# VectorE block transposes in place of TensorE transposes and ScalarE copies in the expert loop of a hybrid decoder step

## The reference, cut to what matters

```python
y = 0
for wg, wu, wd, ge in experts:              # 32 experts, D_MODEL 1024, EXPERT_FF 512
    h = silu(xt @ wg) * (xt @ wu)           # inner activations
    y = y + ge[:, None] * (h @ wd)          # ge: gate of each token for this expert, 0 for most
```

## Time and profile before

| what | value |
| --- | --- |
| time of three runs | 884.41, 885.39, 886.82 us, median 885.39 |
| span of the profiled execution, first to last instruction | 882.0 us |
| TensorE busy in it | 862.2 us (98%) |
| VectorE busy | 350.6 us (40%) |
| ScalarE busy | 180.2 us (20%) |
| expert loop | roughly 390 to 870 us of the span |

### The profile page before, as it was taken

How to read it: one execution, slowest core, us unless ns; L and a number is a source line. 1 busy time by engine, 2 the same in 40 slices (tenths; PEclk the granted TensorE clock), 3 DMA queues, 4 the chain that set the end, 5 groups by cost and what they waited for, 6 DMA issues and landing times.

```text
span 882.0 us, 13906 instructions
## 1 busy us (share of the span) xinstructions
PE 862.2 (98%) x5646; PEld 516.7 (59%) x5646; DVE 350.6 (40%) x816; ACT 180.2 (20%) x362; POOL 30.4 (3%) x89
## 2 busy tenths in 40 slices
PE   8999999999999999999999999999999999999996
PEld 6657777786677667674535553554455445535553
DVE  5476999755577663240102211220222022102214
ACT  3342002347312310131111111110111011101112
POOL 0001203300200000000000000000000000000000
PEclk9999999999999999999999999999999999999998
DMA  7333254114535138909999999999999999999951
GB/s 281 96 95 100 86 176 120 57 43 159 160 112 184 38 144 354 381 28 379 409 419 414 428 416 418 413 430 413 415 418 428 414 414 427 419 417 415 428 229 55
DMA packets 28822, 247.70 MB, mean 281 GB/s; under 512 B 3312, under 2 KB 5616, under 8 KB 16112
## 3 DMA queue, kind: packets, MB, share of 16 engines
q1 hardware_dynamic: 28784, 247.17, 70.6%
HBM read 242.23 MB, written 4.92 MB: 280 GB/s over the span
## 4 chain that ended last, share of the span: by engine, by line
PE 88%; DVE 7%; ACT 2%; DMA 1%; issue 1%; SPq 0%; DVEq 0%; ACTq 0%
PE psum L1121 38%; PE psum L561 13%; PE psum L1074 7%; PE psum L1156 7%; PE psum L572 5%; PE psum L1031 4%; PE psum L1002 1%; PE psum L1078 1%; DVE sb_arena L1692 1%; DVE sb_arena L1689 1%; PE psum L882 1%; PE psum L1139 1%; DMA sb_arena<-w_oab 1%; DMA sb_xT<-xT 1%; PE psum L717 1%
## 5 line engine op out<-in xcount | busy, mean ns | idle before, releaser
L1121 PE MATMUL psum<-sb_arena 128*64 128x512 f32 x1536 | 334.0, 593 | 1.5 <-ACT sb_arena L1462 1.0
L1121 PEld LDWEIGHTS psum<-sb_arena 128*64 128x64 f32 x1536 | 110.9, 136 | 212.6 <-issue 212.6
L2106 DVE TENSOR_TENSOR sb_arena<-sb_arena,psum 128x512 f32<-128x512 f32 x16 | 11.0, 688 | 304.5 <-PE psum L1121 304.5
L561 PE MATMUL psum<-sb_arena 128*128 128x313 f32 (+2 forms) x480 | 126.9, 423 | 0.0
L561 PEld LDWEIGHTS psum<-sb_arena 128*128 128x128 f32 x480 | 90.0, 190 | 34.5 <-issue 2.3
L2101 DVE TENSOR_TENSOR sb_arena<-sb_arena,psum 128x288 f32<-128x288 f32 x120 | 54.5, 454 | 74.8 <-PE psum L1156 71.0
L1074 PEld LDWEIGHTS psum<-sb_arena 128*128 128x128 f32 x544 | 62.0, 192 | 13.6 <-issue 13.0
L572 PE MATMUL psum<-sb_arena 128*128 128x288 f32 x256 | 66.5, 412 | 0.1
L1074 PE MATMUL psum<-sb_arena 128*128 128x128 f32 x544 | 65.2, 278 | 0.4 <-DVE sb_arena L2049 0.4
L1156 PE MATMUL psum<-sb_arena 128*128 128x288 f32 x240 | 61.3, 407 | 0.0
L1455 ACT ACTIVATE sb_arena<-psum 128x256 f32<-128x256 f32 x68 | 20.6, 389 | 179.0 <-PE psum L1078 179.0
(11 more groups left out here) (393 smaller groups left out, 736.4 us busy)
## 6 DMA issues: line engine op xcount, KB each, us to landing
sb_arena<-w_gu SPq DMA_DIRECT2D x64, 2048.0 KB, 15.2
sb_arena<-w_dn SPq DMA_DIRECT2D x32, 2048.0 KB, 11.1
sb_arena<-w_in SPq DMA_DIRECT2D x30, 512.0 KB, 3.6
sb_arena<-w_gab SPq DMA_DIRECT2D x16, 512.0 KB, 3.8
sb_arena<-w_oab SPq DMA_DIRECT2D x16, 256.0 KB, 3.1
sb_arena<-gdn_in SPq DMA_DIRECT2D x4, 512.0 KB, 5.2
sb_arena<-w_o SPq DMA_DIRECT2D x4, 512.0 KB, 6.2
sb_arena<-w_o SPq DMA_DIRECT2D x1, 2048.0 KB, 7.8
```

What stands on the lines that cost most here:

```text
L561: last = mm(bk(n % 2, N)[:, first_col(n):], w_ring[n % 2][:, k, :], (xw if n < 2 else xnT)[:, k, first_col(n):], start=(k == 0), stop=(k = ...
L1121: last = mm(bank[b][half, :], rows[:, k, half], weights(s, k), start=(at_ == 0), stop=(at_ == n_k - 1))
```

## The change

The seven transposes of a pair leave TensorE, and the two copies out of PSUM leave ScalarE. VectorE reads `hid_s` and `selG` in SBUF and writes `hidT` and `selT` in SBUF, in blocks of 32 by 32. One instruction takes 32 partitions and every block column of one kind: four blocks (128 elements per partition) for the activations, three or two blocks (96 or 64 elements) for the gates. Each of the two transposes takes 16 such instructions. `turn_hidden` stands ahead of the adds in VectorE's order, `turn_gates` behind them and ahead of `weigh`.

```diff
 # TensorE
-                    if not first:
-                        pe.wait_ge(S["selT"], i)
                     project(1, KD, xe, ...).then_inc(S["sp_up"], 1)
-                def turn_hidden(i):
-                    pe.wait_ge(S["sp_hid"], i + 1)
-                    for f in range(4):
-                        last = pe.transpose(bank[0][:, f * P:f * P + P], hid_s[:, f * P:f * P + P], K("ident"))
-                    last.then_inc(S["sp_ht"], 1)
-                def turn_gates(i):
-                    pe.wait_ge(S["sp_selg"], i + 1)
-                    for m in range(3):
-                        last = pe.transpose(bank[1][:, m * P:m * P + P], selG[:, m].rearrange("p s c -> p (s c)"), K("ident"))
-                    last.then_inc(S["sp_selT"], 1)
                     gather()
-                    turn_hidden(i)
                     if not first:
                         combine(i, i + 2)
-                    turn_gates(i)
                     down(i, first)
 # ScalarE
                     take(i + 1)
-                    act.wait_ge(S["sp_ht"], i + 1)
-                    A(hidT.rearrange("p k c -> p (k c)"), bank[0][:, :], ACT.Copy).then_inc(S["hidT"], 1)
-                    act.wait_ge(S["sp_selT"], i + 1)
-                    A(selT[:, :], bk(1, 3 * P), ACT.Copy).then_inc(S["selT"], 1)
 # VectorE
+                hid_b = hid_s.rearrange("p (f c) -> p f c", f=4)
+                def turn_hidden():
+                    for b in range(0, P, B32):
+                        for g in range(0, P, B32):
+                            ins = V.transpose(hidT[g:g + B32, :, b:b + B32], hid_b[b:b + B32, :, g:g + B32])
+                    ins.then_inc(S["hidT"], 1)
+                def turn_gates():
+                    to = selT.rearrange("p (m t) -> p m t", m=3)
+                    of = selG.rearrange("p m s c -> p m (s c)")
+                    for b in range(0, P, B32):
+                        n = 2 if b else 3
+                        for g in range(0, P, B32):
+                            ins = V.transpose(to[g:g + B32, 0:n, b:b + B32], of[b:b + B32, 0:n, g:g + B32])
+                    ins.then_inc(S["selT"], 1)
                 def pair(i, first):
                     ...
                     TT(hid_s, silu_s, bank[1][:, :], ALU.mult).then_inc(S["sp_hid"], 1)
+                    dve.wait_ge(S["sp_hid"], i + 1)
+                    turn_hidden()
                     if not first:
                         dve.wait_ge(S["sp_acc"], KD * (i - 1) + 2)
                         add(i)
-                    dve.wait_ge(S["sp_selT"], i + 1)
+                    dve.wait_ge(S["sp_selg"], i + 1)
+                    turn_gates()
+                    dve.wait_ge(S["selT"], i + 1)
                     weigh(i + 1)
```

## The result

The changed kernel takes 880.8 us (median), the one before 885.39: 0.9944 of it, 95% interval 0.993 to 0.9957, so 4 to 6 us faster. I had forecast 899.2 us, 1.6% slower, and 12% for faster. Of the five executions behind the 880.8, one lasted 4981.6 us, which nothing here explains; the other four took 879.31 to 881.83 us, and the ratio and its interval rest on them alone. The profiled execution has a span of 878.1 us, 3.9 less than before.

The account below looks back on a forecast made before the run. TensorE, busy 98%, was taken as the bound; 15 pairs x 0.82 us plus 1.5 for pair 0 gave +13.8 on the 882.0 span, 895.8, plus 3.4 to the median: 899.2 us, range 887 to 915.

Parts of the forecast that it names:

- What VectorE gets: Step pricing VectorE's 32 short block transposes per pair: 0.40 us per activation transpose, taken between 0.39 and 0.42.
- the prediction's own formula: Change per pair with a combine, 16p - 5.58 us: adds' slip less the gate saving; pair 0, 16p - 4.93.
- fixed part: Cost of each VectorE instruction whatever its length: 0.155 us, from elementwise rows, paid every time on part of the partitions.
- The path: Between gather and down projection: ScalarE's copies into `xe` hold combine 2; VectorE's transposes delay the adds that combine 4 needs.
- the activation part: Activation transposes leaving TensorE ahead of the combine: 0 gained in pairs 1 to 15, not 0.59 us.
- the gate part: Gate transposes leaving TensorE between combine and down projection: 0.33 us less per pair in 15 pairs, -4.9 us.
- the signs named for the profile after: Transposes every 0.40 us, ScalarE wait about 0.7, add wait near 1, period 30.9 us, `down` straight after combine, no weight waits.
- the begin of the slip: Combine 4 starts late, waiting for VectorE's first add, by 16p - 5.25 us per pair, positive from p = 0.328.
- cheap short transposes: Rival: p below 0.328 in VectorE's 4.73 us gap, combine 4 not late, 880.0 to 880.8 us; chance 0.10.
- nothing measurable: Rival: p between 0.34 and 0.36, adds' slip and gate saving cancel, 883 to 888 us; chance 0.05.
- Gate transposes on VectorE: After the adds, 16 short transposes taking 4.7 us per pair, covered by TensorE's projections, cost nothing.
- the case of the full 0.92 us: Rival: all TensorE transposes count, 14.7 us less, 870.7 us, but transfers hold it near 875; chance 0.02.

Follow-up runs that it names:

- the run with other shapes: The changed kernel plus block transposes of other shapes and strides into unused space at the end of VectorE's work for a pair: single time 884.28 us.
- the two runs with more transposes: The changed kernel plus two or six further 32x128 transposes per pair ahead of VectorE's sixteen: 887.27 us with two, 909.37 us with six.
- strided ones: The changed kernel with `hid_s` stored interleaved, so the sixteen activation transposes read neighbours four elements apart: 908.28 us, 1.0259 of the kernel before.
- The run with less to transfer: The kernel with six banks, loading only a quarter of the second expert's down weights in each pair after the first: 873.79 us, 0.9868 of the kernel before.
- four banks: The changed kernel with the combine writing banks (6, 7, 0, 1) in place of (6, 7, 2, 3): 879.06 us, 0.9931 of the kernel before.
- six banks: The changed kernel with the combine writing banks (6, 7, 0, 1, 2, 3, 6, 7): 874.44 us, 0.9875 of the kernel before.

## Why the prediction was wrong

**The step that failed is the size p of a short transpose** in "What VectorE gets": 0.40 us, when it is 0.316. In the prediction's own formula each hundredth of a microsecond above 0.328 counts 16 times in each of 15 pairs, and each one in pair 0 counts 16 times: 240 x (0.40 - 0.328) + 16 x 0.084 = 18.6 us, and the forecast of 899.2 lies 18.4 us above the measured 880.8. The size came from the earlier trace rows, whose instructions have the same operation, type and partitions. Their price per element, 1.73 ns, belongs to the stride in their access (`"p c h i -> p i (c h)"` in the code of lines 1701 and 1702), which the row doesn't print, and the new ones read and write runs of 32 adjacent elements. The code was there to be read, and the elementwise rows had the right price per element, 1.04 ns; with it and their fixed part the sum would have been 0.155 + 0.133 = 0.29 us, on the right side of 0.328. The prediction did weigh 1.04 ns per element, but took the 1.93 us of the long row for granted, so that all the rest had to be fixed part (0.87 us) and the case looked absurd. That the long row was dear for its access was not among the possibilities.

**The fixed part and the missing overlap were right.** The earlier trace rows gave 0.155 us and no overlap; measured are 0.17 and a gap of 0.013 us. The reason given, that instructions on a part of the partitions never overlap, is too wide: in the run with other shapes the two 32x512 on the same 32 partitions took 1.29 us together, less than 2 x 0.681. The sixteen of the change go to other partitions from each to the next.

**The path was right.** Combine 2 is held by ScalarE, the activation part gives nothing, the gate part 0.33 us per pair, and the adds are what would be late: all measured by parts. Of the signs named for the profile after, the longer wait for ScalarE came (0.62 us, forecast 0.7), `down` follows the last combine at once, and no load of the loop waits for weights; the wait for an add and the period of 30.9 us, which hung on p, did not come. The formula put the begin of the slip at p = 0.328; the two runs with more transposes put it at 0.316 + 0.30/16 = 0.335.

**The rival "cheap short transposes" came true**: 0.316 lies below its deciding point, 0.328. It had a median of 880.0 to 880.8 us; measured is 880.8. The two traces agree with its terms: the loop is 15 x 0.33 = 4.9 us shorter, pair 0 cost about 0.1 more (from the issue of the gate weights to that of the down weights 20.33 us in place of 20.24), and the loop began 0.8 us later in this execution, before anything that the change touches. That leaves 4.0 us, and the spans differ by 3.9. The match of the totals to a tenth is in part luck. The 3.4 us between span and median do not all lie around the span: each single execution took 1.7 to 1.9 us more than its own span, so the profiled one of the kernel before, at about 883.8 us, was a quick one. The later start and the smaller distance of the changed kernel's median from its span (2.7 us) cancel. Two small slips changed nothing: the formulas give 883.8 to 888.9 us for "nothing measurable", and sizes from 0.328 to 0.34 us had no case of their own.

**The page's 311 ns.** By the page "VectorE: DVE Perf Modes" of the Trainium skill, section "The three transpose paths", the sum was a gain of about 5 us; the trace agrees, with 303 ns on 32 partitions and 312 on 128, in float32. The row that I held against it was of another kind of access. The rule beside it, which gives a 128 by 128 transpose to TensorE where PSUM will do, isn't borne out by this kernel: with the gate transposes on VectorE it took 881.58 us in place of 885.46, because they stood alone on the chain and VectorE was idle; for the activation transposes the choice made no difference (885.5).

**Gate transposes on VectorE** took 4.1 us, not 4.7, and are free as said.

**Clock.** The prediction let no lower clock follow from TensorE's waits, by a gap of 0.95 us in pair 0. In pairs 1 to 15 that held; two stretches of the changed kernel, the first of them the pair before the one shown above, have a granted clock of 1.00 (the number before the last two):

```profile
441.57:471.29 29.72, 29.55 (x162) 13.84 (x164) 14.00 (x46) 3.00 (x7) 0.00 (x0) 1.00 1.00 424
471.29:501.02 29.73, 29.56 (x163) 13.85 (x164) 14.01 (x46) 3.00 (x7) 0.00 (x0) 1.00 1.00 423
```

In pair 0 it did not always hold. There TensorE waits for the transposes ahead of its down projection. In the changed kernel it waited 1.9 us, the clock stayed at 1.00, and the next 96 projection instructions took 20.85 us. With two more transposes it waited 2.6 us, with six more 3.8, with strided ones 3.9. Each time the granted clock then fell to 0.50 to 0.6 over stretches of 2 to 4 us (0.50 is the lower level, 1.2 GHz), and the same 96 instructions took 22.5 us, 1.7 more. The run with less to transfer had this too, after a wait of 2.0 us; the runs with other shapes, four banks and six banks did not, after 1.9. This cost of 1.7 us once is a term that the prediction had at nothing. That the wait brings it about is likely from these traces and not shown: no run varied the wait alone.

**Transfers** were said to hold the case of the full 0.92 us near 875 us. The six-bank version got nearly there with 874.4 and used up the lead over the last five pairs.

## What to carry to other kernels

Before a price is taken from a row with the same operation and shape, compare the strides of both in the code: the row of a profile doesn't show them. Work that is moved to an idle engine is free up to the end of the idle gap and then counts in full. Here 0.30 us were left, and two doses of extra work measured that better than my sum had. And a removed instruction may only have covered a wait: here the 0.59 us came back only when the combine no longer needed the banks that ScalarE was emptying.

## What the runs showed of the hardware

A block transpose of float32 on VectorE costs 0.17 us and 1.03 ns per element when neighbours are adjacent (64 to 1024 elements, 237 to 1225 ns). With source neighbours 32 apart 1024 elements cost 1976 ns and 128 cost 366; with source neighbours 4 apart 128 cost 399. A stride on the destination costs as much as one on the source: lines 1708 and 1713 of the kernel before, 1024 elements each, took 1924 and 1932 ns. An elementwise product of 128x512 that writes with a stride of 4 elements took 1088 ns instead of 688. The sixteen transposes of 32x128, each to other partitions than the one before, don't overlap (one every 0.316 us for 0.303); two of 32x512 on the same partitions took 1.29 us for 2 x 0.681.

In the version with six banks, where a transfer was always pending, the transfers of 2 MB landed 4.91 us apart (66 of them from 513.3 to 837.6 us), 29.5 us for a pair, and a loop of 29.29 us per pair ran on their lead until its last pair, where 0.1 us was lost.

After TensorE had waited 2.0 to 3.9 us for the transposes of pair 0, the granted clock fell to about half, and 96 matmul instructions of 128x512 took 22.5 us instead of 20.85; after waits of 1.9 us, in four traces, it did not fall.
